# A tuned mixer and expert kernel on one core: seven half-size products for the output gate, and the last norm spread over three engines

## What is computed

```python
proj = xn @ w_in
p, u, v, o_pre, if_pre, gates = jnp.split(proj, list(SPLITS), axis=-1)
...
hn = ((h - mu) * lax.rsqrt(var + LN_EPS)).reshape(B, S, MLSTM_WIDTH) * mh_gain
h_out = (jax.nn.sigmoid(o_pre.astype(jnp.float32)) * hn).astype(xn.dtype)
y_mlstm = h_out @ w_branch_mlstm
...
h = layer_norm(DEEPNORM_ALPHA * h + mix, ln1_g[l], ln1_b[l])
ffn = moe_ffn(h, w_router[l], b_router[l], w_e1[l], b_e1[l], w_e2[l], b_e2[l])
h = layer_norm(DEEPNORM_ALPHA * h + ffn, ln2_g[l], ln2_b[l])
```

## Time and profile before

| | us |
|---|---|
| median of 3 runs | 1546.01 (1545.33 to 1546.18) |
| the profiled execution | 1544.39 |
| its span, first to last instruction | 1542.6 |
| TensorE busy | 1410.8 (91%) |
| VectorE busy | 679.6 (44%) |
| ScalarE busy | 154.0 (10%) |
| GpSimd busy | 328.1 (21%) |

### The profile page before, as it was taken

The page is one execution under the profiler, slowest core; times in us unless marked ns, Lnnn a source line. Parts: engine busy times, 40 slices in busy tenths (PEclk is TensorE's granted clock), DMA queues, the critical chain, the costliest instruction groups (busy, mean ns, idle before and its releaser), DMA issues.

```text
span 1542.6 us, 29979 instructions
## 1 busy us (share of the span) xinstructions
PE 1410.8 (91%) x12414; PEld 715.5 (46%) x12415; DVE 679.6 (44%) x1216; ACT 154.0 (10%) x287; POOL 328.1 (21%) x389
## 2 busy tenths in 40 slices
PE   7999999999999998999986788898789899999987
PEld 6887444458874644443332223333233334444442
DVE  5177344333334764354344334443444334434455
ACT  4112322111110120000000000000000000000001
POOL 1060000000000044233323322332233222323210
PEclk9999999999999999999999999999999999999999
DMA  6533100263317599999999999999999999999997
GB/s 220 188 123 102 28 0 1 53 200 96 95 49 307 202 367 416 420 423 422 422 423 423 420 424 424 422 421 423 424 422 422 425 422 424 423 422 420 423 394 273
DMA packets 98102, 478.52 MB, mean 310 GB/s; under 512 B 14820, under 2 KB 61316, under 8 KB 72968
## 3 DMA queue, kind: packets, MB, share of 16 engines
q1 hardware_dynamic: 84064, 457.68, 73.4%
q0 software_dynamic: 12080, 16.64, 3.0%
q10 hardware_dynamic: 1912, 3.56, 0.6%
HBM read 471.17 MB, written 23.08 MB: 320 GB/s over the span
## 4 chain that ended last, share of the span: by engine, by line
PE 70%; DMA 23%; DVE 3%; issue 2%; another core or an unknown queue 1%; ACT 1%; POOL 0%; SPq 0%; DVEq 0%; POOLq 0%; ACTq 0%
PE ps L1962 23%; DMA big<-in_w_e 22%; PE ps L2007 14%; PE ps L1655 12%; PE ps L1858 4%; PE ps L1822 4%; PE ps L1643 3%; PE ps L1739 2%; PE ps L1788 2%; PE ps L1799 2%; PE ps L1757 1%; PE ps L1806 1%; PE ps L1767 1%; DMA rest<-x_rows,P 1%
## 5 line engine op out<-in xcount | busy, mean ns | idle before, releaser
L1962 PE MATMUL ps<-big,rest 128*32 128x512 f32 x5024 | 557.9, 594 | 73.1 <-DMA big<-in_w_e 53.6
L1962 PEld LDWEIGHTS ps<-big,rest 128*32 128x32 f32 x5024 | 167.2, 110 | 448.7 <-issue 439.4
L2007 PE MATMUL ps<-big,rest 128*32 128x256 f32 x4992 | 292.0, 381 | 29.2 <-DMA big<-in_w_e 23.6
L2007 PEld LDWEIGHTS ps<-big,rest 128*32 128x32 f32 x4992 | 174.4, 110 | 154.5 <-issue 50.3
L1484 DVE MEMSET stat<- 128x1 f32 x30 | 1.8, 59 | 468.9 <-PE ps L1962 468.9
L770 POOL DMA_INDIRECT rest<-x_rows,idx x120 | 147.3, 1228 | 57.2 <-issue 31.7
L786 POOL DMA_INDIRECT expert_rows<-rest,slot x120 | 119.2, 994 | 53.9 <-issue 28.4
L1029 ACT ACTIVATE rest<-rest 128x1024 f32<-128x1024 f32 x32 | 33.9, 1060 | 898.5 <-DVE rest L1463 743.0
L778 POOL COPY idx<-P 128x4 uint32 (+1 forms) x30 | 5.5, 185 | 437.7 <-DVE rest L1485 428.6
L746 POOL IOTA P<- 128x128 f32 x1 | 0.2, 243 | 349.8 <-DVE rest L1311 349.8
L1500 DVE TENSOR_TENSOR rest<-ps,rest 128x1024 f32<-128x1024 f32 x32 | 39.2, 1225 | 66.8 <-PE ps L2007 65.8
(11 more groups left out here) (329 smaller groups left out, 1240.0 us busy)
## 6 DMA issues: line engine op xcount, KB each, us to landing
big<-in_w_e SPq DMA_DIRECT2D x187, 2048.0 KB, 24.3
rest<-in_w_in SPq DMA_DIRECT2D x14, 1024.0 KB, 5.5
big<-expert_rows SPq DMA_DIRECT2D x4, 2048.0 KB, 14.7
gate_area<-in_w_in SPq DMA_DIRECT2D x8, 512.0 KB, 4.8
rest<-in_w_in SPq DMA_DIRECT2D x8, 512.0 KB, 4.8
big<-in_w_out SPq DMA_DIRECT2D x1, 4096.0 KB, 12.8
gate_area<-in_w_e SPq DMA_DIRECT2D x2, 2048.0 KB
X<-in_x SPq DMA_DIRECT2D x4, 512.0 KB, 9.4
```

Source lines behind the costliest of these rows:

```text
L1962: last = mm(ps[TB * g:TB * (g + 1), h0 + b, :], rows[:, k, b, :], quarter_of(k, g), start=(k == 2 * order[0]), stop=(k == 2 * order[-1] + 1))
L2007: last = mm(ps[TB * g:TB * (g + 1), 4 + b // 2, YW * (b % 2):YW * (b % 2 + 1)], acts[:, k, b, :], rows_of(k, g), start=(first and k == 0), ...
```

## The change

- The output gate's panel of each head is made by `seven_products`, in banks 0, 1, 5 and 7, with use numbers between those of the wide panels and the branch gates. Its mixed weights and its copies lie in columns of `ucT` that the heads have already read, the third mix in the panel's own place. VectorE makes three of the four mixes after the norm of the head before and the fourth before the next arguments, and the sums before the norm. TensorE waits for all earlier results in banks 0 and 1 to be taken, for the arguments of the next head (bank 5), and before `head_pv` for the sum that reads bank 7. ScalarE makes three copies and then three sigmoids.
- The last norm's rows get tiles of their own, `last_gain` and `last_bias`, and are loaded on SP's queue behind the first expert's four loads. The room comes from the scratch of the software DMA queue, set to 8192 bytes a partition, which is half.
- In the last norm, for the first three tiles, ScalarE multiplies by the root and GpSimd adds the shift; the fourth stays on VectorE, which waits for GpSimd's sums first.
- `mix_weights` is cut into `mix_weights` and `close_mix`; other uses call both in turn. `copy_halves`, `sum_halves` and `seven_products` take their places as arguments. The semaphore `fore_slots` is replaced by a second count of `last_slots`.

```diff
+        last_gain = sb("last_gain", D)
+        last_bias = sb("last_bias", D)
...
+        O_BANKS = (0, 1, 5, 7)
...
+        def use_of_o(h):
+            return N_WIDE + h
...
+        used_uc = [ucT[:, c, :] for c in range(EC + 2)]
+        mix_o = [cut(used_uc[c], 0, HK, P) for c in (0, 1, 2)]
+        part_o = [used_uc[3][:, 0:HALF], used_uc[3][:, HALF:2 * HALF], big[:, SIG_O_AT + S:SIG_O_AT + S + HALF]]
+        assert SIG_O_AT + S + HALF <= MIX_AT
+
+        def o_ring(h):
+            return ring[:, (H + N_WIDE + h) % RING]
+
+        def mixes_of_o(h):
+            return [mix_o[0], mix_o[1], quarters(o_ring(h), True)[2], mix_o[2]]
...
+            sp.wait_ge(norm_rows_landed, 32)
+            sp.dma_start(last_gain[:], A["ln2_g"].broadcast_to([P, D])).then_inc(norm_rows_landed, 16)
+            sp.dma_start(last_bias[:], A["ln2_b"].broadcast_to([P, D])).then_inc(norm_rows_landed, 16)
             load_w2_rows(0, 1)
...
+            pool.wait_ge(norm_rows_landed, 64)
+            for i in range(NT - 1):
+                for n in range(D // BANK):
+                    pool.wait_ge(rows_scaled, 2 * i + n + 1)
+                    t = X0v[:, i, BANK * n:BANK * (n + 1)]
+                    nc.gpsimd.tensor_tensor(t, t, last_bias[:, BANK * n:BANK * (n + 1)], ALU.add).then_inc(out_ready, 1)
...
-                for c in range(EC):
-                    if h >= 1:
-                        act.wait_ge(hout_ready, EC * (h - 1) + c + 1)
-                    take(("o", EC * h + c), sig_o[c], ACT.Sigmoid)
+                copy_halves(use_of_o(h), O_BANKS, part_o)
+                act.wait_ge(gemm_done, at[("o", EC * h + 1)] + 1)
+                if h >= 1:
+                    act.wait_ge(hout_ready, EC * h)
+                act.activation(sig_o[1][:, 0:HALF], ps[:, O_BANKS[0], 0:HALF], ACT.Sigmoid)
+                act.wait_ge(halves_summed, use_of_o(h) + 1)
+                act.activation(sig_o[0], sig_o[0], ACT.Sigmoid)
+                act.activation(sig_o[1][:, HALF:S], sig_o[1][:, HALF:S], ACT.Sigmoid).then_inc(gemm_out, 2)
                 act.preload_act_table_set("natural_log_exp_and_others")
...
-            turn(1)
-            turn(2)
-            act.wait_ge(w2_used, 2 * W2_UNITS)
-            act.dma_start(gain[:], A["ln2_g"].broadcast_to([P, D])).then_inc(norm_rows_landed, 16)
-            act.dma_start(bias[:], A["ln2_b"].broadcast_to([P, D])).then_inc(norm_rows_landed, 16)
-            with act.Fori(3, n_it) as it:
+            with act.Fori(1, n_it) as it:
                 turn(it)
...
+                if i < NT - 1:
+                    act.wait_ge(centred, i + 1)
+                    for n in range(D // BANK):
+                        t = X0v[:, i, BANK * n:BANK * (n + 1)]
+                        act.activation(t, t, ACT.Copy, scale=stat[:, s0 + 14:s0 + 15]).then_inc(rows_scaled, 1)
...
+            def mix_o_panel(h):
+
+                n = H + N_WIDE + h
+                if h == 0:
+                    dve.wait_ge(gemm_done, at[("qk", 2 * EC - 1)] + 1)
+                mix_weights(use_of_o(h), ring_landed[n % RING], 16 * (n // RING + 1), quarters(o_ring(h), True), mixes_of_o(h))
+
+            def close_o_mix(h):
+
+                if h == 0:
+                    dve.wait_ge(gemm_done, at[("qk", 4 * EC - 1)] + 1)
+                close_mix(use_of_o(h), quarters(o_ring(h), True)[1], mixes_of_o(h))
+
+            def sum_o_panel(h):
+
+                if h >= 1:
+                    dve.wait_ge(hout_ready, EC * h)
+                sum_halves(use_of_o(h), O_BANKS, sig_o[0][:, 0:HALF], sig_o[0][:, HALF:S], sig_o[1][:, HALF:S], part_o, part_o[1])
+
             head_args(0)
             head_p(0)
+            mix_o_panel(0)
             for h in range(H):
+                if h >= 1:
+                    close_o_mix(h)
                 if h + 1 < H:
                     head_args(h + 1)
+                    if h == 0:
+                        close_o_mix(h)
                     head_p(h + 1)
                 if h >= 1:
                     head_out(h - 1)
+                sum_o_panel(h)
                 head_norm(h)
+                if h + 1 < H:
+                    mix_o_panel(h + 1)
             head_out(H - 1)
...
-                                                    scalar=stat[:, s0 + 12:s0 + 13], in1=gain[:], op0=ALU.subtract, op1=ALU.mult))
+                                                    scalar=stat[:, s0 + 12:s0 + 13], in1=last_gain[:], op0=ALU.subtract, op1=ALU.mult))
...
                 nc.vector.tensor_tensor(y, y, q, ALU.mult).then_inc(centred, 1)
+                if i < NT - 1:
+                    return
                 dve.wait_ge(centred, i + 1)
+                dve.wait_ge(out_ready, 2 * i)
                 for n in range(D // BANK):
                     t = X0v[:, i, BANK * n:BANK * (n + 1)]
-                    nc.vector.scalar_tensor_tensor(out=t, in0=t, scalar=y, in1=bias[:, BANK * n:BANK * (n + 1)], op0=ALU.mult, op1=ALU.add).then_inc(out_ready, 1)
+                    nc.vector.scalar_tensor_tensor(out=t, in0=t, scalar=y, in1=last_bias[:, BANK * n:BANK * (n + 1)], op0=ALU.mult, op1=ALU.add).then_inc(out_ready, 1)
...
+                if h >= 2:
+                    pe.wait_ge(halves_summed, use_of_o(h - 2) + 1)
...
                 pe.wait_ge(ring_landed[n % RING], 16 * (n // RING + 1))
-                for c in range(EC):
-                    b = bank_for(at[("o", EC * h + c)])
-                    for k in range(KD):
-                        last = mm(ps[:, b, :], ring[:, n % RING][:, k, P * c:P * (c + 1)], h0T[:, k, :], start=(k == 0), stop=(k == KD - 1))
-                    last.then_inc(gemm_done, 1)
+                pe.wait_ge(gemm_out, at[("o", EC * h)])
+                pe.wait_ge(arg_ready, NT * min(h + 2, H))
+                seven_products(use_of_o(h), quarters(o_ring(h), True), O_BANKS, mixed=mixes_of_o(h)).then_inc(gemm_done, 2)
+                pe.wait_ge(top_done, 2 * use_of_o(h) + 2)
                 head_pv(h)
...
-    nc = bacc.Bacc("TRN2", target_bir_lowering=False, num_devices=1)
+    nc = bacc.Bacc("TRN2", target_bir_lowering=False, num_devices=1, dynamic_dma_scratch_size=8192)
```

More of the change, by code:

```diff
@@ L481, in build_program @@
         last_slots = sem("last_slots")
[L482 removed]
+        rows_scaled = sem("rows_scaled")
         last_rows = sem("last_rows")
@@ L873, in take_h0T, with copy_halves @@
                                    scale=gain_col[:, k:k + 1], bias=bias_col[:, k:k + 1]).then_inc(h0T_ready, 1)
-            def copy_halves(q, banks):
+            def copy_halves(q, banks, into=part):
                 for n in range(3):
@@ L879, in copy_halves @@
                         act.wait_ge(halves_summed, q)
-                    act.activation(part[n], ps[:, banks[0], 0:HALF], ACT.Copy).then_inc(sum_copied, 1)
+                    act.activation(into[n], ps[:, banks[0], 0:HALF], ACT.Copy).then_inc(sum_copied, 1)
             def take_wide(q, n, dst):
@@ L1144, in mix_weights, with close_mix, sum_halves @@
                     dve.wait_ge(part_done, 3 * q)
[L1145 removed]
+                nc.vector.tensor_tensor(mixes[0], w21, w22, ALU.add).then_inc(mix_w_ready, 1)
                 dve.wait_ge(mix_w_ready, 4 * q + 1)
[L1147 to L1148 removed]
+                nc.vector.tensor_tensor(mixes[1], mixes[0], w11, ALU.subtract).then_inc(mix_w_ready, 1)
+                nc.vector.tensor_tensor(mixes[2], w11, w21, ALU.subtract).then_inc(mix_w_ready, 1)
+            def close_mix(q, w12, mixes=mix_w):
                 dve.wait_ge(mix_w_ready, 4 * q + 2)
[L1150 to L1152 removed]
+                nc.vector.tensor_tensor(mixes[3], w12, mixes[1], ALU.subtract).then_inc(mix_w_ready, 1)
+            def sum_halves(q, banks, top_early, top_late, low_late, parts=part, total=part_sum):
                 dve.wait_ge(part_done, 3 * q + 2)
                 dve.wait_ge(sum_copied, 3 * q + 2)
[L1156 to L1157 removed]
+                nc.vector.tensor_tensor(top_early, parts[0], ps[:, banks[1], 0:HALF], ALU.add).then_inc(top_done, 1)
+                step(nc.vector.tensor_tensor(total, parts[1], ps[:, banks[2], 0:HALF], ALU.add))
                 dve.wait_ge(part_done, 3 * q + 3)
[L1159 removed]
+                nc.vector.tensor_tensor(top_late, total, ps[:, banks[3], 0:HALF], ALU.add).then_inc(top_done, 1)
                 dve.wait_ge(sum_copied, 3 * q + 3)
[L1161 removed]
+                nc.vector.tensor_tensor(low_late, parts[2], ps[:, banks[2], 0:HALF], ALU.add).then_inc(halves_summed, 1)
             def mix_panel(q):
@@ L1644, in v_product, with seven_products @@
                 last.then_inc(gemm_done, 1)
-            def seven_products(q, w, banks, operand=(h0_first, h0_second, mix_h, 0)):
+            def seven_products(q, w, banks, operand=(h0_first, h0_second, mix_h, 0), mixed=mix_w):
                 w11, w12, w21, w22 = w
@@ L1662, in seven_products @@
                 pe.wait_ge(mix_w_ready, 4 * q + 1)
```

(8 more changed lines are left out.)

13 lines of the change are left out of this document (8 added, 5 removed).

## The result

The changed kernel takes 1538.21 us in the median of five runs beside the kernel before's 1546.01: a ratio of 0.9945, 95% interval 0.9932 to 0.9958. In two later comparisons, each with runs of the kernel before on the same chip, it came out at 0.9937 (0.9923 to 0.9951, median 1536.12) and 0.9937 (0.9923 to 0.9950, median 1535.60). By the medians it is 7.8 to 10.7 us faster, by the ratios 8.5 to 9.7. The forecast was 1537.3, 8.7 us. One run of the kernel before (1840.56 us at a granted clock of 0.752) and one of the gate panels alone (2447.5 us at 0.557) were slow, and the ratios here leave them out.

The account below looks back on a forecast made before the run. TensorE was taken to bound the kernel before 540 us, then matmuls and the full weight stream by its bytes. Gains of 5.1 + 2.5 + 1.1 = 8.7 us from 1546.01 gave 1537.3, range 1535.0 to 1541.8.

Parts of the forecast that it names:

- The limits of the stretches: Whole kernel: TensorE time saved before 460 us advances everything behind it equally; bytes removed behind 560 save their transfer time.
- The panels: Output gate, four heads: 1.65 us gained each, 0.5 lost for heads 1 to 3 awaiting both transposed halves; 5.1 us.
- rival D: Head stage: seven products stall on VectorE or ScalarE, 1 us or more a head; 1541 to 1543 us; chance 0.10.
- The rows: Last norm's row loads leave the full stream for SP's idle queue: 1.05 MB less, 2.5 us gained, bounds 0 to 2.7.
- The last norm: Tail: relieving VectorE gives 1.1 us, not 4.2, because norm 3 waits for its transfer; bounds 0 to 1.3.
- GpSimd beside VectorE: Last norm: VectorE's short steps could each lose 0.7 us to GpSimd's sums in norms 1 and 2, hidden by waiting.
- The scratch: Indirect DMAs on half the scratch: 0 expected; at worst 0.5 us on each of four scatters, 2 us.
- rival F: GpSimd waits for earlier indirect DMAs to land: about 1930 us, or 18 us in a milder form, 1555; chance 0.06.
- The sum: Whole kernel: 8.7 us gained, 10.6 with each term at its upper bound, 1.1 at its lower; 1537.3 us.

Follow-up runs that it names:

- gate panels alone: The kernel before with only the seven-product gate panels added; rows, last norm and scratch as before: median 1539.62 us, 0.9960 of before.
- split wait: Changed kernel with TensorE's wait for both transposed halves cut in two, the second before the first product writing bank 1: median 1534.99 us, 0.9928 of before.
- held stores: Changed kernel with SP holding every result store until the fourth load of expert rows has landed: median 1536.17 us, 0.9940 of before.

## Why the prediction was right

The predicted time lies 0.9 us under the first median and 1.2 and 1.7 us over the two others, inside the range each time. The steps:

- **The limits of the stretches.** Right. The 4.9 us by which the first expert load comes earlier (5.3 counted from the first gate panel) are there at the landing near 810 (gate panels alone: 5.7 or more) and at the rows' loads (5.5 or more).
- **The panels: 4 x 1.65 less 3 x 0.5, 5.1 us.** Right in both parts: 13.81 to 12.16 us a panel, and 0.44 us lost behind the transposes in place of 0.5. The sum of the measured parts is 4 x 1.65 - 3 x 0.44 = 5.3, and the first load, counted from the first gate panel, is 5.24 to 5.28 us earlier. The split wait gives the second part back, so it was that wait. VectorE's sums fitted where they were put, with 0.57 us to spare ahead of the arguments and 1.34 ahead of the norm; rival D did not come.
- **The rows: 2.5 us.** Right in mechanism, a little large: 2.1 us by the medians, 1.9 to 2.6 by the landing. The two rows' transfer behind the first expert's loads costs nothing at the place where SP waits 56 us anyway.
- **The last norm: 1.1 us, not 4.2.** Right that VectorE is no longer the limit: it waits 1.79 us before norm 3. The size was short: it is 1.3 to 2.1 us, at or above the upper bound of 1.3. The mis-sized term is the arrival of norm 3's sums, taken from the one trace at hand with its 0.91 us wait for the fourth load. In the traces of the changed kernel TensorE's own chain sets it: 5.49 us of matmuls from the start of norm 2's last product to that of norm 3's, 1519.49 to 1524.98, begun when the third load has landed, where the kernel before has 6.46 (1525.47 to 1531.93). The prediction held that no edit touches the four loads; the fourth lands 1.4 us closer behind the third in every trace with the new gate panels. That the stores caused it was my second guess, and it fell with the held stores.
- **GpSimd beside VectorE.** In norm 1 a refinement step takes 0.43 us where it takes 0.22 in the others, and it ends at 1520.70, where GpSimd's two sums end (1518.18 + 2.51 = 1520.69). All seven traces in which GpSimd adds have one such step of norm 1 at 0.43, ending within 0.03 us of GpSimd's sums, and the five others have none. That is 0.2 us, less than the 0.7 given for it, and it lies ahead of idle time. It fits the exclusive lock of the Trainium skill ("SBUF — State Buffer", section "SBUF: two separate sides"), by which whichever of the two engines starts first holds the shared ports for the whole instruction and the other is blocked; steps that fall only on the end of a sum do not prove it. A centring step with one input in PSUM ran beside the same sums at its usual 1.27 us.
- **The scratch: 0.** Right at half. The price in rival F was too high where such waits do show: at a sixteenth, ten more of them in some 250 indirect DMAs than before, of at most 2.4 us, and one of them on the path.
- **The sum.** That it came so close is partly luck. The measured terms are 5.3, 2.1 and 1.3 to 2.1, together 8.7 to 9.5 us: the rows were 0.4 too large and the norm up to 1.0 too small, and the two offset each other. In rival D a loss of 1 us a head leaves 4.7 us, not 4, or 1541.3, which changes nothing in the forecast.

## What to carry to other kernels

Where a transfer stream is full from some point on, a microsecond saved before it and the bytes taken out of it are both worth most or all of their size (here 5.3 us and 2.1 of 2.5); a relieved engine in the tail is worth only the distance to what arrives next, so look up that arrival before counting the relief. A wait for a transfer that one kernel's trace shows can be gone in the edited kernel, even where no edit touches the transfer: the 0.91 us here stood in all three traces without the new panels, at 0.42 to 0.91, and in none of the nine with them. So give such a bound a range of its own, down to the matmul chain in front of the product that waits. When operands are shared in banks, put the wait for a bank in front of the product that writes it and not in front of the first one.

## What the runs showed of the hardware

With four gathers and four scatters of 128 rows a round, GpSimd's indirect DMAs run on half of the scratch at a ratio of 0.9999, and on a sixteenth at 1.0011, where 14 of some 250 stand behind an unexplained idle time of 0.4 to 2.4 us, against 4 before. The last of the same four loads of expert rows landed 20.8 to 23.3 us after its issue in twelve traces, and which end of that a kernel gets did not depend on the stores beside it; the three late ones had a 16 KB packet of the `instruction` queue beside them, the nine others none. In a float32 kernel a VectorE step with two small SBUF inputs took 0.43 us in place of 0.22 where it met the end of a GpSimd sum, in all seven traces that have such sums.
